# VectorE takes over the rows of the last four condition weights of a hybrid encoder layer

## The reference

```
mod = (silu(c) @ w_ada + b_ada).reshape(bsz, 6, 2048)      # w_ada: 2048 x 12288
shift1, scale1, gate1, shift2, scale2, gate2 = mod
h = rmsnorm(x, norm1_g) * (1 + scale1) + shift1
u, v, z, xbc, dt_raw = split(h @ w_in)                      # w_in: 2048 x 5136
gm_out  = chunk_mlp(gelu(u), gelu(v))                       # spatial gating, 8 heads
ssm_out = mamba_ssd(silu(causal_conv(xbc)), z, dt_raw)      # 16 heads, chunks of 64 in the reference
x = x + gate1 * (concat(gm_out, ssm_out) @ w_out)
h = rmsnorm(x, norm2_g) * (1 + scale2) + shift2
x = x + gate2 * hier_moe(h)                                 # 16 experts, 2 per token
```

## Time and profile before

| | before |
|---|---|
| median of 3 runs | 1315.39 us (1311.54 to 1320.19) |
| profiled execution, its own time | 1320.46 us |
| span from its first to its last instruction | 1318.7 us |
| TensorE busy | 1194.1 us, 91% of the span |
| VectorE busy | 298.1 us, 23% |
| ScalarE busy | 200.3 us, 15% |
| mean DMA rate | 306 GB/s, 404.18 MB |
| mean granted TensorE clock | 0.960 |

### The profile page before, as it was taken

How to read it: one execution, slowest core, us unless ns; L and a number is a source line. 1 busy time by engine, 2 the same in 40 slices (tenths; PEclk the granted TensorE clock), 3 DMA queues, 4 the chain that set the end, 5 groups by cost and what they waited for, 6 DMA issues and landing times.

```text
span 1318.7 us, 14948 instructions
## 1 busy us (share of the span) xinstructions
PE 1194.1 (91%) x6096; PEld 636.8 (48%) x6097; DVE 298.1 (23%) x669; ACT 200.3 (15%) x393; POOL 71.6 (5%) x122
## 2 busy tenths in 40 slices
PE   4888999999999999999999399979987998799995
PEld 1445556545455444545555245544554455445541
DVE  2001402212122223102114611211121112111127
ACT  4011201113112223011111101110111011101102
POOL 1003000010000000010000000000000000000000
PEclk9998999999999999999999599989999999999996
DMA  9999776877656457593632678999999999999982
GB/s 329 389 388 381 238 296 273 318 285 324 261 226 278 193 224 288 201 351 135 235 128 90 228 278 334 388 411 427 396 409 409 417 365 407 410 425 373 412 262 80
DMA packets 82479, 404.18 MB, mean 306 GB/s; under 512 B 6364, under 2 KB 8684, under 8 KB 53598
## 3 DMA queue, kind: packets, MB, share of 16 engines
q1 hardware_dynamic: 74032, 372.26, 72.6%
q0 software_dynamic: 7456, 28.52, 6.1%
q10 hardware_dynamic: 944, 2.74, 0.6%
HBM read 392.24 MB, written 21.94 MB: 314 GB/s over the span
## 4 chain that ended last, share of the span: by engine, by line
PE 73%; DMA 20%; DVE 3%; SPq 2%; issue 1%; ACT 1%; POOLq 0%; DVEq 0%; ACTq 0%
PE bank L864 21%; DMA arena<-in_w_gate_dram 12%; PE bank L1268 9%; PE bank L1265 7%; PE bank L949 6%; DMA arena<-in_w_ada_dram 6%; PE bank L868 5%; PE bank L859 4%; PE bank L1292 4%; PE bank L1289 3%; PE bank L900 2%; DMA arena<-in_w_up_dram 2%; PE bank L880 1%; SPq L340 1%; PE bank L1249 1%
## 5 line engine op out<-in xcount | busy, mean ns | idle before, releaser
L864 PE MATMUL bank<-arena 128*128 128x512 f32 x640 | 288.5, 601 | 0.0
L1265 PE MATMUL bank<-arena 128*64 128x256 f32 x1536 | 174.9, 387 | 25.1 <-DMA arena<-in_w_gate_dram 14.7
L864 PEld LDWEIGHTS bank<-arena 128*128 128x128 f32 x640 | 118.8, 191 | 135.6 <-issue 134.6
L1265 PEld LDWEIGHTS bank<-arena 128*64 128x64 f32 x1536 | 111.2, 139 | 92.6 <-DMA arena<-in_w_gate_dram 18.7
L1268 PE MATMUL bank<-arena 128*128 128x512 f32 x256 | 114.2, 608 | 8.9 <-DMA arena<-in_w_gate_dram 7.8
L1289 PE MATMUL bank<-arena 128*64 128x512 f32 x384 | 85.0, 595 | 6.0 <-DVE arena L1841 6.0
L949 PE MATMUL bank<-arena 128*128 128x320 f32 x320 | 87.4, 433 | 0.0
L1268 PEld LDWEIGHTS bank<-arena 128*128 128x128 f32 x256 | 49.5, 195 | 73.0 <-issue 62.5
L1838 DVE SCALAR_TENSOR_TENSOR arena<-bank,arena 128x512 f32<-128x512 f32 x16 | 12.0, 751 | 304.5 <-PE bank L1265 185.8
L949 PEld LDWEIGHTS bank<-arena 128*128 128x128 f32 x320 | 60.4, 190 | 27.8 <-issue 3.2
L868 PE MATMUL bank<-arena 128*64 128x256 f32 x640 | 73.5, 382 | 0.0
(11 more groups left out here) (347 smaller groups left out, 870.8 us busy)
## 6 DMA issues: line engine op xcount, KB each, us to landing
arena<-in_w_ada_dram SPq DMA_DIRECT2D x48, 2048.0 KB, 14.7
arena<-in_w_gate_dram SPq DMA_DIRECT2D x32, 2048.0 KB, 21.2
arena<-in_w_up_dram SPq DMA_DIRECT2D x32, 2048.0 KB, 21.2
arena<-in_w_down_dram SPq DMA_DIRECT2D x32, 2048.0 KB, 20.8
arena<-in_w_in_dram SPq DMA_DIRECT2D x16, 2048.0 KB, 8.0
arena<-in_w_out_dram SPq DMA_DIRECT2D x8, 2048.0 KB, 11.1
arena<-in_w_in_dram SPq DMA_DIRECT2D x4, 1536.0 KB, 18.4
arena<-mod_final POOLq DMA_DIRECT2D x6, 1024.0 KB, 19.0
```

The costliest lines, as they stand in the source:

```text
L864: return mm(bank[:, :], lhsT=xT_[:, t, OFF[j]:OFF[j] + P], rhs=w, start=start, stop=stop)
L1265: last = mm(PB[bank][64 * h:64 * h + 64, 0:HALF], lhsT=XeT[:, t0 + t, 0:64], rhs=slots_w[count][:, t, HALF * h:HALF * h + HALF], start=sta ...
```

## The change

TensorE no longer multiplies the rows of m = 2 to 5. A row is now loaded by itself, 1 MB, into one of three places: two in slot A1 and a third in a region that is free at the time (a fourth stands for the third from step k = 10 on). VectorE multiplies it by the condition value of each partition and adds it to one of two sums of 128 x 2048 (`ada_sum`, in slot A0), one sum per stream: two instructions per row, 128 in all, of which the first two of each modulation are plain multiplications (`tensor_scalar`) and the other 120 multiply and add (`scalar_tensor_tensor`, two tensor inputs). `STEP_ROWS` says how many of the 64 rows belong to each half step k = 2n - 2 + half: 1, 1, 3, 3, then 4 each, and 5, 5, 6 at the end. For n = 1 to 3 the rows stand ahead of the convolutions of channel groups 6, 8 and 12; from n = 4 on half of a step's instructions stand ahead of the hooks of each quarter. At the end of a modulation (k = 5, 9, 13 and 16) TensorE adds each sum over the partitions with a one-hot stationary operand: eight matmuls of 128 x 32 by 512. The end of m = 5 moves from n = 8, second half, to n = 9, first half, and that of m = 2 from n = 2 to n = 3.

SyncE's order becomes: the first two rows of a step, the W half, the other rows of the step. A row waits until the row three before it has been added (`ada_acc`), and at row 32 for GpSimd's stores of zeros (`side_stored`). The first two `w_out` halves wait for the last sum (`ada_summed`). Three semaphores are merged into others, with the same order as before, and `vsq` lies elsewhere.

```
+        ada_sum = [at(2 * SLOT, D), at(2 * SLOT + D, D)]
+        row_place = [at(3 * SLOT, D), at(3 * SLOT + D, D), at(MX + 3072, D), at(MX, D)]
+        one_hot = br_spare[:, 0:33]
...
-        uses_before = {E0: 0, E1: 0, A0: 22, A1: 22, W0: 15, W1: 15}
+        uses_before = {E0: 0, E1: 0, A0: 6, A1: 6, W0: 15, W1: 15}
+        loads_before = {E0: 0, E1: 0, A0: 28, A1: 27, W0: 15, W1: 15}
...
+        ada_acc, ada_summed = map(sem, ("ada_acc", "ada_summed"))
+        row_in = [slot_in[A0], slot_in[A1], wc_in[0]]
...
+        STEP_ROWS = ("V", "V", "VVV", "VVV", "VVVV", "VVVV", "VVVV", "VVVV", "VVVV", "VVVV",
+                     "VVVV", "VVVV", "VVVV", "VVVV", "VVVVV", "VVVVV", "VVVVVV")
+        row_by = "".join(STEP_ROWS)
+        row_step = [k for k, by in enumerate(STEP_ROWS) for _ in by]
+        assert len(row_by) == 4 * KT
+
+        def rows_of(k, by):
+
+            return [(r, row_by[:r].count(by)) for r in range(4 * KT) if row_step[r] == k and row_by[r] == by]
+
+        def ends_in(k):
+
+            return next((2 + r // KT for r in range(KT - 1, 4 * KT, KT) if row_step[r] == k), None)
+
+        def place_of(r):
+            return row_place[r % 3 if r % 3 < 2 or row_step[r] < 10 else 3]
+
+        def row_loads(r):
+            return r // 3 + 1 + (4 if r % 3 < 2 else 2)
...
-            def ada(slot, m, k):
-                sp.dma_start(slots_ada[slot], w_ada_v[:, 2 * k:2 * k + 2, bass.ds(m * D, D)]).then_inc(slot_in[slot], 16)
+            def ada_row(r):
+
+                m, t = 2 + r // KT, r % KT
+                if r >= 3:
+                    sp.wait_ge(ada_acc, 2 * r - 4)
+                sp.dma_start(place_of(r), w_ada_v[:, t, m * D:m * D + D]).then_inc(row_in[r % 3], 16)
...
-            sp.wait_ge(slot_used[A0], 4)
-            ada(A0, 2, 0)
-            sp.wait_ge(slot_used[A1], 4)
-            ada(A1, 2, 1)
             sp.wait_ge(slot_used[W1], 4)
             win_half(W1, 1)
-            for n in range(1, 9):
-                i, c = (n - 1) // 2, (n - 1) % 2
-                sp.wait_ge(slot_used[W0], 4 + n)
-                win(W0, n + 1, 0)
-                for a, k in ((A0, 2), (A1, 3)):
-                    sp.wait_ge(slot_used[a], 3 + 2 * n)
-                    ada(a, 2 + i, 4 * c + k)
-                sp.wait_ge(slot_used[W1], 4 + n)
-                win(W1, n + 1, 1)
-                if n < 8:
-                    for a, k in ((A0, 0), (A1, 1)):
-                        sp.wait_ge(slot_used[a], 4 + 2 * n)
-                        ada(a, 2 + i + c, 4 * (1 - c) + k)
-
-            sp.wait_ge(slot_used[A0], 20)
+            sp.wait_ge(slot_used[A1], 4)
+            r = 0
+            for k in range(17):
+
+                for behind in (False, True):
+                    if behind and k:
+                        slot, n = (W0, W1)[(k - 1) % 2], (k - 1) // 2 + 1
+                        sp.wait_ge(slot_used[slot], 4 + n)
+                        win(slot, n + 1, (k - 1) % 2)
+                    while r < 4 * KT and row_step[r] == k and (behind or row_step[r - 2:r].count(k) < 2):
+                        if row_step[r] == 10 and row_step[r - 1] == 9:
+                            sp.wait_ge(side_stored, 112)
+                        ada_row(r)
+                        r += 1
+
+            sp.wait_ge(ada_summed, 4)
             wout(A0, 0, 0)
-            sp.wait_ge(slot_used[A1], 20)
             wout(A1, 0, 1)
-            for q, (a, b, na, nb) in enumerate(((W0, W1, 13, 13), (A0, A1, 21, 21), (W0, W1, 14, 14)), 1):
+            for q, (a, b, na, nb) in enumerate(((W0, W1, 13, 13), (A0, A1, 5, 5), (W0, W1, 14, 14)), 1):
...
+            def modrow_move(m):
+
+                buf = m % 2
+                act.wait_ge(ada_summed, m - 1)
...
+                if n == 3:
+                    modrow_move(2)
                 if n == 2:
-                    modrow_move(2, 0, 8)
...
-                        if n in (4, 6, 8):
-                            if n > 4:
-                                act.wait_ge(mod_stored, 16 * n - 32)
-                            modrow_move(n // 2 + 1, n // 2 % 2 ^ 1, 4 + 2 * n)
+                    if quarter % 2:
+                        m = ends_in(2 * n - 2 + quarter // 2)
+                        if m:
+                            modrow_move(m)
...
-            def ada(slot, t0):
-
-                for t in (t0, t0 + 1):
-                    for j in range(4):
-                        last = mm(PB[7][32 * j:32 * j + 32, :], lhsT=cT[:, t, 2:34], rhs=slots_ada[slot][:, t - t0, j * N:j * N + N],
-                                  start=(t == 0), stop=(t == KT - 1))
-                last.then_inc(slot_used[slot], 1)
+            def ada(k):
+
+                m = ends_in(k)
+                if m:
+                    pe.wait_ge(modrow_out, m + 3)
+                    pe.wait_ge(ada_acc, 2 * KT * (m - 1))
+                    for b in range(2):
+                        for j in range(4):
+                            last = mm(PB[7][32 * j:32 * j + 32, :], lhsT=one_hot[:, 1 - b:33 - b], rhs=ada_sum[b][:, j * N:j * N + N],
+                                      start=(b == 0), stop=(b == 1))
+                    last.then_inc(ada_summed, 1)
...
-                    if n % 2 and half == 0:
-                        pe.wait_ge(modrow_out, 5 + n // 2)
-                    for a, slot_a in ((0, A0), (1, A1)):
-                        arrived(slot_a, 2 * n + 3 + half)
-                        ada(slot_a, 8 * ((n - 1) % 2) + 4 * half + 2 * a)
+                    ada(2 * n - 2 + half)
...
+            step(V.memset(one_hot, 0.0))
+            step(V.memset(one_hot[:, 1:2], 1.0))
...
+            def ada(k, part=slice(None)):
+
+                for r, i, b in [(r, i, b) for r, i in rows_of(k, "V") for b in range(2)][part]:
+                    m, t = 2 + r // KT, r % KT
+                    if b == 0:
+                        dve.wait_ge(row_in[r % 3], 16 * row_loads(r))
+                    c, w = cT[:, t, 2 + b:3 + b], place_of(r)
+                    if "V" not in row_by[r - t:r]:
+                        if m == 2:
+                            dve.wait_ge(slot_used[A0], 4)
+                        else:
+                            dve.wait_ge(ada_summed, m - 2)
+                        V.tensor_scalar(ada_sum[b], w, c, None, ALU.mult).then_inc(ada_acc, 1)
+                    else:
+                        dve.wait_ge(ada_acc, 2 * i + b - 1)
+                        V.scalar_tensor_tensor(ada_sum[b], w, c, ada_sum[b], ALU.mult, ALU.add).then_inc(ada_acc, 1)
+
             for ch in range(16):
+                if ch in (6, 8, 12):
+                    k = {6: 0, 8: 2, 12: 4}[ch]
+                    ada(k)
+                    ada(k + 1)
...
+                    if 2 * n - 2 + quarter // 2 < len(STEP_ROWS):
+                        n_rows = len(STEP_ROWS[2 * n - 2 + quarter // 2])
+                        ada(2 * n - 2 + quarter // 2, slice(n_rows, None) if quarter % 2 else slice(0, n_rows))
```

More of the change, by code:

```diff
@@ L162, in trunk @@
         st = take(96)
-        br = take(2, 20)
+        br_spare = take(40)
+        br = br_spare.rearrange("p (b e) -> p b e", b=2)
         R1 = ptr[0]
@@ L171, in trunk @@
         wc[0] = at(MX, 4, 768)
-        vsq = at(MX, 1024)
+        vsq = at(PR, 1024)
         SA = MX + 5120
@@ L272, in trunk @@
         wc_in = [sem(f"wc{k}_in") for k in range(2)]
-        a_ready, dt_abs, Ye_free = map(sem, ("a_ready", "dt_abs", "Ye_free"))
+        ada_acc, ada_summed = map(sem, ("ada_acc", "ada_summed"))
+        row_in = [slot_in[A0], slot_in[A1], wc_in[0]]
+        Ye_free = sem("Ye_free")
         rows_read = sem("rows_read")
@@ L591, in _ @@
             pool.sem_inc(routed, 1)
-            pool.wait_ge(slot_used[A1], last_visit + 23)
+            pool.wait_ge(slot_used[A1], last_visit + 7)
             pool.sem_inc(routed, 1)
@@ L620, in _, with modrow_out_of_bank @@
                 act.activation(cT[:, :, 2 + b], craw[:, b, :], ACT.Silu).then_inc(cT_ready, 1)
-            def modrow_out_of_bank(buf, used):
-                act.wait_ge(slot_used[A1], used)
+            def modrow_out_of_bank(buf):
                 act.activation(modrow[:, buf, :], PB[7][:, :], ACT.Copy).then_inc(modrow_out, 1)
-            def modrow_move(m, buf, used):
-                modrow_out_of_bank(buf, used)
+            def modrow_move(m):
+                buf = m % 2
+                act.wait_ge(ada_summed, m - 1)
+                if m > 3:
+                    act.wait_ge(mod_stored, 32 * m - 64)
+                modrow_out_of_bank(buf)
                 act.wait_ge(modrow_out, m + 4)
@@ L641, in _ @@
                     act.wait_ge(modT, q - 1)
-                modrow_out_of_bank(q % 2, q + 1)
+                act.wait_ge(slot_used[A1], q + 1)
+                modrow_out_of_bank(q % 2)
                 act.wait_ge(mod_ready, q + 1)
@@ L667, in _ @@
             act.wait_ge(small_in, 160)
-            act.activation(hb[:, 1, :], hb[:, 1, :], ACT.Exp).then_inc(a_ready, 1)
```

(25 more changed lines are left out.)

## The result

The changed kernel takes 1349.41 us (median of 4 runs, 1347.73 to 1355.02), against 1313.47 us before (4 runs, 1311.36 to 1320.19): a ratio of 1.0272, 95% interval 1.0244 to 1.0301, slower. Its profiled execution took 1348.59 us with a span of 1346.9 us, 28.2 more than the span before.

A forecast was written before the change was run, and what follows sets the result against it. TensorE set the pace before; VectorE's adds would after. Last add 20.6 us later, sum 1.8, clock 2 and `mf` 2 make 26.4; 1320.5 + 26.4 = 1346.9, less 5.1 to the median, gives 1342 us; range 1314 to 1374.

The forecast's parts named there:

- Price of an add: VectorE's row instructions: 2.28 us per add and 1.21 per multiplication from start to start, 283.3 us in all.
- VectorE as the bound: From 141.5 us to the last add: 375.6 us of VectorE work plus waits, ending at 562.8, 20.6 later than before.
- Fixed: VectorE's remaining waits for channel groups 6 and n = 2's, and for dt: 19.6 us together.
- hand-offs: VectorE's waits in the hooks for TensorE's transposes or products and ScalarE's results: 19.4 us, from 0 to twice that.
- late rows: Adds waiting for rows not landed: 6.7 us; as a rival, 40 us on top, 1382 us, chance 0.14.
- Sums: TensorE's eight matmuls at each modulation's end: 1.8 us each, 7.2 for four, the last 1.8 on the path.
- The projection: Start of the output projection: 26.4 us later than before, at about 594 us.
- The way in stages: Through the half steps: n = 4 starts at about 240 us against 255.4, n = 8 some 6 early, n = 9 level.
- SyncE's queue: no price: Loads of W halves behind rows: 26 us in hand for a transfer of 8, so no cost.
- The end follows one for one: Expert stage after the output projection: a shift of the projection shifts the kernel's end by the same amount.
- level: Rival: hand-offs and late rows cost nothing, so +0, 1315 us; chance 0.17.
- TensorE stays the bound: Rival: the adds fill only VectorE's idle time, so 42 to 57 us off, some 1266 us; chance 0.11.

The follow-up runs named there:

- the shared kernel: Against the changed kernel, 18 of the 64 rows go back to TensorE, row by row; 1289.5 us, ratio to before 0.981.
- The run that took that wait away: Against the changed kernel, SyncE issues each step's W half ahead of all its rows; 1350.7 us, ratio to before 1.028.
- the other four complete kernels: Against the changed kernel: hooks ahead of adds, 1365.6 us; W half first, 1350.7; 18 rows back on TensorE, 1289.5; two fewer such rows, 1295.6.
- the half rows: Against the changed kernel, each row's transfer brings 1024 columns and each add reads them twice; median 1328.5 us, projection start 593.0 against 596.4.

## Why the prediction was right

The forecast was 1342 us and the result 1349.4, slower for the reason given. Some of the closeness is luck: VectorE's work came out 3.9 us below its term and its waits 7.6 above. Point by point:

- **Price of an add: right.** 273.4 us for 120 and 9.9 for 8 single-input ones are 283.3 us, the sum predicted from two rows of two instructions each. Start to start it is 2.26 us, where 2.28 was taken (ten adds in 22.71 us at 160.7; less the last one's 2.34 and divided by nine).
- **VectorE as the bound: right.** 375.6 us of work were predicted, and 425.0 less 53.3 of waits are 371.7. The experiments with 1536 and 1024 columns and with one input move the start by the price of an add alone, by 38 to 63 us.
- **Waits: right in kind, a little short.** Fixed 19.6, measured 21.7; hand-offs 19.4, measured 24.2; late rows 6.7, measured 7.4. The 8 us for group 6 came out (8.1) although the two rows ahead of it end at 148.4 and not 150.5: their first two instructions are the cheap form, and the group came 2 us earlier too. The hand-offs are the mis-sized term (4.8 of the 7.6). The largest was ScalarE's exponential for the third tile (L1538), 7.3 us where 3.9 stood. Work and waits together put the last add at 566.5 instead of 562.8.
- **Sums: mis-sized, and the clock with them.** 1.8 us each were predicted; behind a wait they took 3.4 to 3.6, at a granted clock of 0.50, the lower level (0.54 in the first). Where TensorE came to them without a long wait, in the shared kernel, the first three took 1.9; the fourth, behind five rows with short waits, took 3.6 at 0.50. The prediction had the clock, but behind the sum, as 2 us of the matmuls that follow, with 2 more for `mf`. From the end of the sum to the projection it is 26.2 us where it was 25.5 before: 0.7 instead of 4. That is the `gm1` matmuls, 2.73 us instead of 2.05; `mf` cost nothing. So 3.6 + 0.7 stand for 1.8 + 4. The Trainium skill (TensorE: Matmul & The Clock Gate, "Part 1") has a clock that is throttled until activity releases it; the 0.50 behind the waits here agrees.
- **The projection:** 24.3 us (last add), 3.7 (sum) and 0.7 make 28.7, forecast 26.4.
- **The way in stages: right.** n = 4 at 240 predicted, 240.8 measured; n = 8 some 6 us early, 467.4 against 473.1; n = 9 level, 522.3 against 523.0. TensorE's waits, "about 10 us each and 26 at the last", were 9.4, 11.0, 7.3 and 22.5.
- **"SyncE's queue: no price": wrong, without consequence.** The half for n = 5 took 22.9 us from issue to landing and TensorE waited 2.1 for it. The run that took that wait away gained nothing, but it made rows late instead.
- **Not foreseen:** TensorE waited 8.5 us at n = 9 for ScalarE, which `ln` held (L733), and 6.1 at `sb` for VectorE. The first is VectorE's lateness too: ScalarE had waited 10.3 us for VectorE's first step of `ln` (L1614), which came at 514.2, behind five adds. Both lie ahead of a longer wait for adds, which would take up what they cost; that is argued, as no run takes one of them away and leaves the rest.
- **The end follows one for one: right here,** 28.2 for 28.7. From the start of the projection to the end it is 751.0 us before and 750.5 with the change, but 745.9 to 749.4 in the other four complete kernels, with the same division of the experts; so it holds to 5 us.
- **The rest of the miss,** 7.4 us in all: 2.3 are the projection. The other 5 are the step from a profiled execution to the median: the one of before lay 5.1 us above the median of that time (7.0 above the later one), the one of after 0.8 below. Executions of before ran from 1307.65 to 1321.86, so this is not a finding, and where the medians' further 7.8 us lie stays open.
- **Two slips without consequence.** The terms of the upper bound add up to 1371 us (1315.4 + 26.4 + 9 + 20), not 1374; and row 32, of k = 10, is four half steps behind the stores of zeros during n = 4, not six.

The rivals: *late rows* is out by the half rows, *level* by the hand-offs, which are real (24.2 us). *TensorE stays the bound* would have needed adds at the price of one input, and with these the start is 33.8 us ahead of before. The rival had given 42 to 57 us for it: with cheap adds VectorE waits 41.5 us for rows, and TensorE still waits 14.9 for adds at the end of m = 5 and 6.9 for the W half at n = 5. That rival had left out the rows.

## What to carry to other kernels

An engine with 77% of its time free has room for work of that price only as far as its waits can be filled; price the moved work by a row of the same form, number of tensor inputs included, and add its fixed waits before calling it free. When two engines can do the same thing, divide it so that both arrive together: here 18 of 64 rows left with TensorE turn 2.7% slower into 1.9% faster. And when an experiment changes values, ask whether anything later depends on them (here, which expert runs how) and compare a point ahead of that.

## What the hardware showed

- **VectorE's price is a line.** With two tensor inputs 1280, 1811 and 2344 ns for 1024, 1536 and 2048 columns: 1.04 ns a column and some 216 ns besides. With one input 748, 1013 and 1279 ns: 0.52 ns a column and the same 217. (The one-input figures are the means of the eight first-row multiplications in the kernels with 1024 and 1536 columns and in the changed one.)
- **Neighbours overlap by 0.08 us** even when one reads what the one two before it wrote: 2.344 us long, 2.26 from start to start.
- **Stores and loads at the same time.** At 272.9 us GpSimd issues five 1 MB stores of zeros, which before went out at 291.2. They go through GpSimd's queue and the rows through SyncE's. With them in flight a row took 21.2 us to land, instead of the median of 5.3, and the W half ahead of it in the queue 22.9, instead of 9.9. The DMA engines were 97% busy at 378 GB/s (columns as in the earlier trace rows):

```profile
268.00:303.00 35.00, 26.76 (x106) 15.04 (x105) 28.09 (x17) 7.06 (x11) 4.47 (x6) 0.85 0.97 378
```

The chain of the changed kernel there:

```profile
278.88 16.74 DMA arena<-in_w_ada_dram
295.62 4.58 issue
300.20 2.41 DVE arena L1473 x2
```

Both pieces are the one row's transfer: 16.74 us until VectorE was done with its hooks, and 4.58, VectorE's wait, which the chain books as "issue". This is where VectorE lost 4.6 of its 7.4 us for rows. That the stores are the cause is argued from the coincidence; no run takes them away.
